# Peer input regrouped by four tokens, read in one, two, four and eight rounds

## The chip, the cores and the metric

The kernel runs on one core of one Trainium2 chip. The metric is the device time of one execution in microseconds. The kernel before takes 1576.94 us (median of three runs, 1575.91 to 1576.96).

## The reference, cut to what matters

Two transformer blocks of width 1024 run over 256 tokens. The first ends with a PEER layer: each of 8 heads picks 16 of 16384 experts per token, and an expert is one row of `peer_u` and one of `peer_v`.

```python
u = peer_u[ec]
a = jax.nn.gelu(jnp.einsum("ckd,cd->ck", u, hc).astype(jnp.float32)) * gc
vv = peer_v[ec]
out = jnp.einsum("ck,ckd->cd", a.astype(vv.dtype), vv)
```

The kernel gathers nothing: it multiplies the normed input `h` by all 16384 rows of `peer_u` (the "scores"), applies gelu, multiplies by gates that are zero for experts not chosen, and then multiplies by all of `peer_v` (the "values").

## The kernel before, in words

**Products.** Every large product is made in three parts with fp32r operands: weights and activations are each split into a rounded part and a rest, and the sum is w_hi x h_hi + w_hi x h_lo + w_lo x h_hi. Weights come from HBM in tiles of 128 x 1024 floats. Two tiles make a chunk, which fills one PSUM bank (`gemm0` to `gemm3`, in rotation). For each tile `product_tile` (L669 to L689) issues 8 matmuls of w_hi with h_hi and 8 with h_lo (L683), then 8 of w_lo with h_hi (L688). In each, the stationary operand is 128 x 128 weights and the moving operand 128 partitions x 256 tokens of one of the 8 parts k of h. A chunk is 48 matmuls.

**Order of the moving operand.** A helper reorders both the moving operand and the PSUM output of every such matmul:

```python
def spread(tile):
    return tile.rearrange("p (j g c) -> p g j c", g=4, c=4)
```

The 256 tokens are taken as 64 groups of four neighbours. The matmul goes through them in 4 rounds of 16 groups, and within a round from every fourth group to the next: 64 bytes on in SBUF and 64 bytes on in PSUM. A group of four floats is 16 bytes. `h_hi` and `h_lo` are two tiles of 8 x 256 floats per partition, so part k begins 1024 bytes after part k-1.

**The scores stage.** There are 64 chunks of `peer_u`. Four chunks, one for each PSUM bank, make one round of a hardware loop (`expert_scores`, L942, for the first 32 chunks; the loop at L970 to L975 for the other 32, in which the small f16 matmuls of `gate_planes`, L966, come before every second chunk). SP loads raw tiles, ACT rounds them to w_hi (L1368) and applies gelu to the finished bank (L1556). The rest w_lo is made by POOL (L466) in the first 32 chunks and by DVE (L466) in the other 32. Each waits by semaphores for the tile before it.

**Where h comes from.** During the eight peer query chunks, which run on another copy (`g_parts`), DVE forms the normed h in `sq` (L2187), ACT rounds it to `h_hi` in four pieces of 128 x 512 (`round_h(1)`, L1322), and DVE subtracts to get `h_lo` in four pieces (`norm2_rest`, L2178). In DVE's queue these subtractions stand between the evacuations of the query banks (L2183); in ACT's queue the roundings stand between roundings of weights. After the query chunks TensorE scores the keys (L936), waits for all pieces of h and starts the scores stage.

Of the kernel before, what the change touches and what calls it, by code (L numbers as in the profile page):

```python
# [30 lines left out]
F32R = mybir.dt.float32r  # L31
# [3 lines left out]
ALU = mybir.AluOpType  # L35
ACT = mybir.ActivationFunctionType
AX = mybir.AxisListType

P = 128
T = 256  # L40
TT = T // P
D = 1024
KD = D // P
# [4 lines left out]
BANKS = 4  # L48
CW = 256
GROUP = 8  # L50
GATE_PARTS = 2
GATE_SCALE = 2.0 ** 14


CONV_W = 31
# [111 lines left out]
def build(nc, t):  # L167
    plan, order = plan_chunks()
    ctx = ExitStack()
    with ctx:  # L170
        def sb(name, shape, dt=F32):
            return ctx.enter_context(nc.sbuf_tensor(name, shape, dt))

        def sem(name):
            return ctx.enter_context(nc.semaphore(name))


        gemm = [ctx.enter_context(nc.psum_tensor(f"gemm{i}", [P, 512], F32)) for i in range(BANKS)]
        aux = [ctx.enter_context(nc.psum_tensor(f"aux{i}", [P, 512], F32)) for i in range(4)]

        def pair(bank, rows=P):
            return bank[0:rows, :].rearrange("p (n t) -> p n t", n=2)
# [3 lines left out]
        w_hi = [sb(f"w_hi{v}", [P, TILE], F32R) for v in range(2)]  # L186
        w_lo = [sb(f"w_lo{v}", [P, TILE], F32R) for v in range(2)]
        xres = sb("xres", [P, KD, T])
        with nc.sbuf_tensor("act_parts", [P, KD, T], F32R) as act_parts:
            pass  # L190
        sb("ahead_of_h", [P, 8])
        h_hi = sb("h_hi", [P, KD, T], F32R)
        with nc.sbuf_tensor("mem_sq", [P, KD, T], F32) as mem_sq:
            pass
        h_lo = sb("h_lo", [P, KD, T], F32R)
        sb("behind_h", [P, 8])
        std = sb("std", [P, T])
        rstd = sb("rstd", [P, T])
        params = sb("params", [P, NPAR])
# [48 lines left out]
        sq = carve(KD, T)  # L248
# [47 lines left out]
            "p b n (g i o) -> p b n g i o", g=GROUP // 2, o=2)  # L296
        hot2 = carve(2, GROUP // 2 * P * 2, dt=F16).rearrange("p b (g i o) -> p b g i o", g=GROUP // 2, o=2)

        a_hi, a_lo = [act_parts[:, i:i + 4, :].rearrange("p (c v) t -> p c v t", c=2) for i in (0, 4)]
        memT = small[:, 0:KD * T].rearrange("p (k t) -> p k t", t=T)  # L300

# [73 lines left out]
        hi_ready = [sem(f"hi_ready{v}") for v in range(2)]  # L375
        lo_ready = [sem(f"lo_ready{v}") for v in range(2)]
        hi_used = [sem(f"hi_used{v}") for v in range(2)]
        tile_done = [sem(f"tile_done{v}") for v in range(2)]
# [53 lines left out]
        def spread(tile):  # L432

            return tile.rearrange("p (j g c) -> p g j c", g=4, c=4)

        def by_k(tile, m, rows=P, n=KD):

            return tile[0:rows, 0:n * m].rearrange("p (k m) -> p k m", m=m)
# [51 lines left out]
        HALF = P // 4  # L490
# [166 lines left out]
        def _(pe):  # L657
            def product(c, m, it=None, x=(h_hi, h_lo), steps=KD):

                for v in range(2):  # L660
                    product_tile(c, v, m, it, x, steps)

            def bank_free(c, it=None):
                if it is not None:
                    pe.wait_ge(evacuated[c.bank], it + (c.bank_use - 1))
                elif c.bank_use > 1:
                    pe.wait_ge(evacuated[c.bank], c.bank_use - 1)
# [23 lines left out]
            def paced_product(c, m, rounded, split, before, x=(h_hi, h_lo), step=2):  # L691


                bank_free(c)
                both = pair(gemm[c.bank], m)
                hi, lo = [by_k(w, m) for w in w_hi], by_k(w_lo[0], m)
# [156 lines left out]
            for k in range(2):  # L853
                mm = pe.matmul(aux[2][:, 0:T], ones[:, :], sq[:, k, :], start=(k == 0), stop=(k == 1))
# [42 lines left out]
            for k in range(KD // 2):  # L897
                mm = pe.matmul(aux[3][:, 0:T], ones[:, :], sq[:, k, :], start=(k == 0), stop=(k == KD // 2 - 1))
# [3 lines left out]
            for j in range(HEADS + 1):  # L902
                if j and j + 1 < HEADS:
                    scores(j + 1)
                if j:
                    turn_probs(j - 1)
                    name, i, v = beside_heads[j - 1]
# [20 lines left out]
            for g in range(TT * 4):  # L928
# [5 lines left out]
                for i in range(4):  # L934
                    v, at = divmod(h0 + i, HALVES // 2)
                    mm = pe.matmul(aux[g % 4][:, i * NK:(i + 1) * NK], qp[:, h0 + i, tt * P:(tt + 1) * P],  # L936
                                   raw[kc.raw][v][:, at * NK:(at + 1) * NK], start=True, stop=True)
# [3 lines left out]

            def expert_scores(first, last):  # L942
                with pe.Fori(first, last) as it:
                    for c in plan["u"][:BANKS]:
                        product(c, P, it)

            pe.wait_ge(h_rounded, 16)
            pe.wait_ge(h_split, 16)
            expert_scores(0, ROUTED + 1)

            pe.wait_ge(gates_ready, 1)
            for n, src in enumerate((e1, e2, sc)):
                for tt in range(TT):
                    mm = pe.transpose(aux[n][:, tt * P:(tt + 1) * P],
                                      src[:, tt].rearrange("p h k -> p (h k)"), ident[:, :])
# [14 lines left out]
            with pe.Fori(0, ITS // 2) as it:  # L970
                for s in range(BANKS):
                    if s % 2 == 0:
                        gate_planes(0, s, it)
                        gate_planes(0, s + 1, it)
                    product(plan["u"][HALF + s], P, it)  # L975

            def expert_values(c, it, opens=False):
                for v in range(2):
# [103 lines left out]
            for h in range(GH):  # L1082
                mm = pe.matmul(pair(aux[h // 2], GDK)[:, h % 2, :], wdec[:, h, :], dec, start=True, stop=True)
# [5 lines left out]
            for h in range(K96):  # L1089
                if h in MQ_TILES:  # L1090
                    n = MQ_TILES.index(h)
# [56 lines left out]
            for tt in range(TT):  # L1148
                for h in range(GH):
                    mm = pe.transpose(aux[tt][:, h * GDK:(h + 1) * GDK], ekd[:, h, tt * P:(tt + 1) * P],  # L1150
                                      ident[0:GDK, 0:GDK])
# [4 lines left out]
            for h in range(GH):  # L1156
                for n in range(NCH):
                    lo, cols = (n % 2) * GCHUNK, slice(n * GCHUNK, (n + 1) * GCHUNK)
                    at_col = (h * TT + n // 2) * GCHUNK
                    mm = pe.matmul(aux[2][lo:lo + GCHUNK, at_col:at_col + GCHUNK], emg[:, h, cols],  # L1160
                                   eg[:, h, cols], start=True, stop=True)
# [99 lines left out]
            for i, c in enumerate(plan["down"]):  # L1261
                pr, g = divmod(i, 3)
# [3 lines left out]
                for v in range(2):  # L1266
                    out = gemm[1][:, 0:T] if pr == 3 and v else pair(aux[pr])[:, v, :]
                    for w, x, ready in ((w_hi, f_hi, hi_ready), (w_hi, f_lo, hi_ready), (w_lo, f_hi, lo_ready)):
                        pe.wait_ge(ready[v], c.split + 1)
                        for k in range(KD):  # L1270

                            mm = pe.matmul(spread(out), w[v][:, k * P:(k + 1) * P], spread(x[:, g * KD + k, :]),  # L1272
                                           start=(g == k == 0 and (v == 0 or pr == 3) and w is w_hi and x is f_hi),
                                           stop=(g == 2 and w is w_lo and k == KD - 1), skip_group_check=True)
# [6 lines left out]
            for part in (0, KD - 1):  # L1281
# [3 lines left out]
                for tt in range(TT):  # L1285
                    mm = pe.matmul(last_sums[:, tt:tt + 1], sq[:, part, tt * P:(tt + 1) * P], ones[:, 0:1],
                                   start=(part == tt == 0), stop=(part == KD - 1), skip_group_check=True)
            mm.then_inc(sumsq, 1)
            keep_warm(3)
            for tt in range(TT):  # L1290
                pe.wait_ge(rstd_done, 7 + tt + 1)
                mm = pe.matmul(last_rstd[:, tt * P:(tt + 1) * P], ones[:, :], spread_rstd[:, tt, :], start=(tt == 0),
                               stop=(tt == TT - 1), skip_group_check=True)
# [4 lines left out]
        def _(act):  # L1298
# [16 lines left out]
            def round_h(j, beside=None):  # L1315

                for q in range(4):
                    part = slice(2 * q, 2 * q + 2)
                    if beside:
                        beside(q)  # L1320
                    act.wait_ge(h_ready, 4 * j + q + 1)
                    act.activation(h_hi[:, part, :], pair(NORMED[q]) if j == 2 else sq[:, part, :],  # L1322
                                   ACT.Copy).then_inc(h_rounded, 1)

# [84 lines left out]
            for n in range(4):  # L1409
                part = slice(2 * n, 2 * n + 2)  # L1410
# [59 lines left out]
            for half in range(2):  # L1470
                part = slice(4 * half, 4 * half + 4)
# [38 lines left out]
            for j in range(HEADS + 3):  # L1510
# [9 lines left out]
                if j in Y_STEPS:  # L1520
                    part = slice(4 * Y_STEPS.index(j), 4 * Y_STEPS.index(j) + 4)
                    act.wait_ge(conv_act, 1)
                    act.activation(y_hi[:, part, :], zv[:, part, :], ACT.Copy).then_inc(y_rounded, 1)
                if j < HEADS:
                    name, i, v = beside_heads[j]
# [10 lines left out]
            for i in range(4):  # L1536
                part = slice(2 * i, 2 * i + 2)
# [130 lines left out]
            c = plan["dec"][0]  # L1668
# [83 lines left out]
            for u in range(MH * QB):  # L1752
# [4 lines left out]
                if u and u % 2 == 0:  # L1757
                    c = plan["gate0"][u // 2 - 1]
# [8 lines left out]
            c = plan["gate0"][-1]  # L1767
# [66 lines left out]
            for i in range(4):  # L1834
                look_ahead(plan["branch1"][i].index + 1)
                act.wait_ge(merge_done, 4 + i + 1)
                part = slice(2 * i, 2 * i + 2)
# [64 lines left out]
        def _(dve):  # L1902
# [227 lines left out]
            for j in range(HEADS + 3):  # L2130
# [6 lines left out]
                if j in Y_STEPS:  # L2137
                    half = Y_STEPS.index(j)
                    part = slice(4 * half, 4 * half + 4)
# [7 lines left out]
                if j >= 11 and j % 2:  # L2147
                    i = (j - 11) // 2
                    c = plan["conv_out"][i]
# [3 lines left out]
                    part = ga[:, 2 * i:2 * i + 2, :]  # L2153
# [21 lines left out]
            def norm2_rest(q):  # L2175
                part = slice(2 * q, 2 * q + 2)
                dve.wait_ge(h_rounded, 12 + q + 1)
                dve.tensor_tensor(h_lo[:, part, :], sq[:, part, :], h_hi[:, part, :], ALU.subtract).then_inc(h_split, 1)  # L2178

            both = rstd[:, :].unsqueeze(1).to_broadcast([P, 2, T])  # L2180
            for i, c in enumerate(plan["peer_q"]):
# [81 lines left out]
            for n, (dst, done) in enumerate(((e1T, planes_used[0]), (e2T, planes_used[1]), (gT, routed))):  # L2263
                dve.wait_ge(routed_psum, n + 1)
                if dst is gT:
                    dve.tensor_scalar(dst, aux[n][:, 0:T], GATE_SCALE, None, ALU.mult).then_inc(done, 1)
                else:
# [32 lines left out]
            def apply_gates(half, s, it):  # L2300
# [3 lines left out]
                                bass.ds(it * (BANKS * GROUP) + GROUP * s, GROUP)]  # L2304
                dve.scalar_tensor_tensor(part, aux[b][:, :].rearrange("p (t i) -> p i t", t=GROUP), 1.0 / GATE_SCALE,  # L2305
                                         part, ALU.mult, ALU.mult).then_inc(planes_used[b], 1)
# [47 lines left out]
            for q in range(4):  # L2354
                part = slice(2 * q, 2 * q + 2)
# [8 lines left out]
            for b in range(BANKS):  # L2364
                dve.wait_ge(experts_turned, b + 1)
                part = xres[:, 2 * b:2 * b + 2, :]
# [287 lines left out]
            for pr in range(3):  # L2654
                taken(dve, plan["down"][3 * pr + 2])
                part = xres[:, 2 * pr:2 * pr + 2, :]
                dve.tensor_tensor(part, part, pair(aux[pr]), ALU.add).then_inc(x4_done, 1)
                gather_squares(6, pr)
            c = plan["down"][-1]
# [15 lines left out]
            for first, last in OUT_TILES:  # L2675
                part = yout[:, first:last, :]
# [92 lines left out]
```

## Time and profile before

| | us |
|---|---|
| median of the runs | 1576.94 |
| the profiled execution's own time | 1579.04 |
| its span (first to last instruction) | 1577.0 |
| TensorE busy | 1561.8 (99%) |
| scores stage, from its first matmul to the first of the values stage | 326.90 to 699.88 |

The profile gives each engine's busy time, groups of instructions by source line, and a chain of waits: it starts at the last instruction and goes back at each step to what released it, or to the instruction before it on the same engine. Where that chain stays on one engine, the time is that engine's own pace, and the length of a piece divided by its instructions is the time from one start to the next. The duration of a single matmul is longer than that, because matmuls overlap.

### The profile page before, as it was taken

The page shows a single profiled execution, that of the slowest core. Times are in us where ns is not written, and L with a number is a line of the kernel's source. Part 1 is how long each engine was busy: PE and PEld are TensorE (multiplying, and loading weights), DVE is VectorE, ACT ScalarE, POOL GpSimd, SP SyncE. Part 2 cuts the span into 40 slices and gives each one's busy share as a digit, 9 for nine tenths or more (in the row PEclk, how much of TensorE's full clock was granted, in tenths as well). Part 3 has the DMA queues.
Part 4 walks back from the last instruction along what each step waited for, and adds up shares of the span by engine and source line. Part 5 has one row for each costly group of instructions (what it writes and reads, how often), then busy time and mean ns, then how long its engine had stood idle before and what let it go on. Part 6 is the DMA issues. An engine that isn't in the chain of part 4 may idle for free.

```text
span 1577.0 us, 33476 instructions
## 1 busy us (share of the span) xinstructions
PE 1561.8 (99%) x12568; PEld 1472.4 (93%) x12568; DVE 1070.0 (68%) x1867; ACT 881.5 (56%) x1251; POOL 883.0 (56%) x413
## 2 busy tenths in 40 slices
PE   9999999999999999999999999999999999999998
PEld 8999899999999999998888888889999999999998
DVE  7998743869933777778888666776937484455522
ACT  5566775554454444444444445557677654676653
POOL 7786458968886000000000244458875689888886
PEclk9999999999999999999999999999999999999999
DMA  6565345656656555555555666666543356666664
GB/s 211 173 199 164 95 134 186 188 181 193 188 186 191 179 164 183 172 166 172 185 177 170 215 195 189 192 202 188 180 140 111 118 165 189 195 195 191 188 193 127
DMA packets 86217, 277.03 MB, mean 176 GB/s; under 512 B 11232, under 2 KB 18160, under 8 KB 86128
## 3 DMA queue, kind: packets, MB, share of 16 engines
q1 hardware_dynamic: 85712, 274.76, 55.8%
q8 instruction: 59, 0.97, 0.3%
q0 software_dynamic: 272, 1.05, 0.2%
q14 instruction: 30, 0.25, 0.1%
q10 hardware_dynamic: 144, 0.00, 0.0%
HBM read 274.73 MB, written 1.05 MB: 175 GB/s over the span
## 4 chain that ended last, share of the span: by engine, by line
PE 91%; POOL 2%; issue 2%; DVE 2%; ACT 2%; DMA 1%; SPq 0%; DVEq 0%; ACTq 0%; POOLq 0%
PE gemm L683 35%; PE gemm L986 22%; PE gemm L688 18%; PE aux L1272 4%; PE gemm L817 3%; PE aux L966 2%; POOL w_lo L466 2%; PE gemm L704 1%; PE gemm L729 1%; ACT w_hi L1368 1%; PE gemm L1272 1%; PE aux L936 0%; PE gemm L803 0%; PE gemm L746 0%; PE gemm L710 0%
## 5 line engine op out<-in xcount | busy, mean ns | idle before, releaser
L466 POOL TENSOR_TENSOR w_lo<-raw,w_hi 128x1024 fp32r<-128x1024 f32 (+1 forms) x330 | 789.7, 2403 | 284.8 <-ACT w_hi L1368 283.9
L1368 ACT ACTIVATE w_hi<-raw 128x1024 fp32r<-128x1024 f32 (+1 forms) x492 | 515.0, 1048 | 560.9 <-PE gemm L683 309.0
L683 PE MATMUL gemm<-h_hi,w_hi 128*128 128x256 f32 x2096 | 289.3, 280 | 1.1 <-ACT w_hi L1368 1.0
L683 PE MATMUL gemm<-h_lo,w_hi 128*128 128x256 f32 x2144 | 289.9, 277 | 0.0
L688 PE MATMUL gemm<-h_hi,w_lo 128*128 128x256 f32 x2096 | 284.4, 277 | 2.6 <-POOL w_lo L466 1.8
L683 PEld LDWEIGHTS gemm<-h_lo,w_hi 128*128 128x128 f32 x2144 | 265.9, 188 | 0.3 <-issue 0.2
L683 PEld LDWEIGHTS gemm<-h_hi,w_hi 128*128 128x128 f32 x2096 | 261.1, 188 | 4.2 <-issue 1.6
L688 PEld LDWEIGHTS gemm<-h_hi,w_lo 128*128 128x128 f32 x2096 | 260.0, 188 | 5.0 <-POOL w_lo L466 3.6
L466 DVE TENSOR_TENSOR w_lo<-raw,w_hi 128x1024 fp32r<-128x1024 f32 x162 | 195.6, 1222 | 101.4 <-ACT w_hi L1368 100.4
L986 PE MATMUL gemm<-w_hi,act_parts 128*128 128x512 f32 x1008 | 249.0, 387 | 0.4 <-ACT act_parts L1569 0.4
L986 PEld LDWEIGHTS gemm<-w_hi,act_parts 128*128 128x128 f32 x1008 | 187.7, 188 | 37.6 <-issue 0.5
L627 POOL DMA_DIRECT2D small<-in_memT x1 | 1.0, 1029 | 379.1 <-DVE big L2305 379.1
L986 PE MATMUL gemm<-w_lo,act_parts 128*128 128x512 f32 x504 | 134.0, 386 | 0.0
L2311 DVE TENSOR_TENSOR act_parts<-big,act_parts 128x512 fp32r<-128x512 f32 x64 | 89.2, 1394 | 47.5 <-ACT act_parts L1569 47.3
L986 PEld LDWEIGHTS gemm<-w_lo,act_parts 128*128 128x128 f32 x504 | 94.4, 187 | 19.5 <-DVE w_lo L466 0.3
L2048 DVE SCALAR_TENSOR_TENSOR aux<-big,params,aux 128x256 f32<-128x256 f32 x240 | 94.8, 506 | 0.0
L462 POOL TENSOR_TENSOR w_lo<-raw,w_hi 128x768 fp32r<-128x768 f32 x30 | 59.2, 1974 | 17.5 <-ACT w_hi L1365 16.7
L2297 DVE TENSOR_TENSOR small<-small 128x512 f16<-128x512 f16 x128 | 57.1, 488 | 0.0
L2614 DVE SCALAR_TENSOR_TENSOR big<-gemm,params,big 128x255 f32<-128x255 f32 (+1 forms) x96 | 39.7, 476 | 24.6 <-ACT big L1851 24.6
L2294 DVE TENSOR_TENSOR small<-small 128x1024 f16<-128x1024 f16 x64 | 43.8, 685 | 0.0
L2305 DVE SCALAR_TENSOR_TENSOR big<-aux,big 128x512 f32 x64 | 41.0, 683 | 0.0
L1569 ACT ACTIVATE act_parts<-big 128x512 fp32r (+1 forms) x64 | 40.0, 627 | 0.2 <-issue 0.2
(436 smaller groups left out, 2047.5 us busy)
## 6 DMA issues: line engine op xcount, KB each, us to landing
raw<-in_w_u SPq DMA_DIRECT2D x128, 512.0 KB, 4.0
raw<-in_w_ev SPq DMA_DIRECT2D x128, 512.0 KB, 3.9
raw<-in_w_up SPq DMA_DIRECT2D x48, 512.0 KB, 4.3
raw<-in_w_gate SPq DMA_DIRECT2D x24, 512.0 KB, 3.8
raw<-in_w_down SPq DMA_DIRECT2D x24, 512.0 KB, 4.3
raw<-in_w_conv_in SPq DMA_DIRECT2D x16, 512.0 KB, 4.4
raw<-in_w_peer_q SPq DMA_DIRECT2D x16, 512.0 KB, 4.3
raw<-in_w_branch SPq DMA_DIRECT2D x24, 288.0 KB, 2.9
```

Source lines behind the costliest of these rows:

```text
L462: eng.tensor_tensor(lo[:, :, 0:C96], by_k(raw[c.raw][v], C96), hi[:, :, 0:C96], ALU.subtract)
L466: eng.tensor_tensor(w_lo[v][:, 0:n], raw[c.raw][v][:, 0:n], w_hi[v][:, 0:n], ALU.subtract).then_inc(lo_ready[v], 1)
L683: mm = pe.matmul(spread(out), w[:, k, :], spread(act_part[:, k, :]), start=(n == k == 0), stop=False)
L688: mm = pe.matmul(spread(out), w[:, k, :], spread(x[0][:, k, :]), start=False, stop=(k == steps - 1))
L817: mm = pe.matmul(spread(pair(gemm[c.bank])[:, tt, :]), x[:, v * KD // 2 + k, tt * P:(tt + 1) * P], spread(w[:, k, :]), start=(begins and t ...
L986: mm = pe.matmul(spread(gemm[2 * half + tt][:, :]), a[:, c.raw, v, tt * P:(tt + 1) * P], spread(w[v][:, half * (D // 2):(half + 1) * (D // ...
L1272: mm = pe.matmul(spread(out), w[v][:, k * P:(k + 1) * P], spread(x[:, g * KD + k, :]), start=(g == k == 0 and (v == 0 or pr == 3) and w is ...
L1368: act.activation(w_hi[v][:, 0:n], raw[c.raw][v][:, 0:n], ACT.Copy).then_inc(hi_ready[v], 1)
L2048: ins = dve.scalar_tensor_tensor(acc, zc[:, k, w:w + T], tap, acc, ALU.mult, ALU.add)
L2294: dve.tensor_tensor(hot2[:, b], each(iota2, P), along(e2T[:, tokens], P), ALU.is_equal)
L2297: ins = dve.tensor_tensor(hot1[:, b, part], hot[:, b], along(gate_parts[:, part, tokens], P // 2), ALU.mult)
L2311: dve.tensor_tensor(a_lo[:, c.raw, :, :], act_peer[:, plane, :], a_hi[:, c.raw, :, :], ALU.subtract).then_inc(a_split, 1)
```

## The change: what it does

The two parts of h for the scores stage get a tile of their own layout, `peer_h`, over the place of `h_hi` and `h_lo`. It has 64 groups, 272 bytes from group to group (`PITCH` 17 x 16 bytes). In a group stand four tokens of h_hi for k = 0 to 7, then four of h_lo for k = 0 to 7, then 16 bytes unused. ACT and DVE write it directly in this order. The spacer behind h grows by 1024 bytes, and what is allocated after it moves by as much.

`score_product` takes the place of `product` in the scores stage. It has the same 48 matmuls in the same sequence with the same waits, but the first, second, third and fourth chunk of each round of the loop go through the 64 groups in 1, 2, 4 and 8 rounds. The steps from group to group are then 272, 544, 1088 and 2176 bytes in SBUF and 16, 32, 64 and 128 bytes in PSUM. Other products keep `spread`.

```diff
+PITCH = 17
+ROUNDS = (1, 2, 4, 8)
...
+        with nc.sbuf_tensor("peer_h", [P, T // 4 * PITCH * 4], F32R) as peer_h:
+            pass
         h_hi = sb("h_hi", [P, KD, T], F32R)
...
-        sb("behind_h", [P, 8])
+        sb("behind_h", [P, 264])
...
+        peer_parts = [peer_h[:, :].rearrange("p (g k c) -> p k g c", k=PITCH, c=4)[:, n * KD:(n + 1) * KD]
+                      for n in range(2)]
...
+            def score_product(c, it, rounds):
+
+                bank_free(c, it)
+                for v in range(2):
+                    out = pair(gemm[c.bank])[:, v, :].rearrange("p (j g c) -> p g j c", g=rounds, c=4)
+
+                    def one(w, part, k, begins=False, ends=False):
+                        moving = peer_parts[part][:, k].rearrange("p (j g) c -> p g j c", g=rounds)
+                        return pe.matmul(out, w[:, k, :], moving, start=begins, stop=ends)
+
+                    pe.wait_ge(hi_ready[v], it * BANKS + (c.split + 1))
+                    for part in range(2):
+                        for k in range(KD):
+                            mm = one(by_k(w_hi[v], P), part, k, begins=(part == k == 0))
+                    mm.then_inc(hi_used[v], 1)
+                    pe.wait_ge(lo_ready[v], it * BANKS + (c.split + 1))
+                    for k in range(KD):
+                        mm = one(by_k(w_lo[v], P), 0, k, ends=(k == KD - 1))
+                    mm.then_inc(tile_done[v], 1)
...
-                    for c in plan["u"][:BANKS]:
-                        product(c, P, it)
+                    for s, c in enumerate(plan["u"][:BANKS]):
+                        score_product(c, it, ROUNDS[s])
...
-                    product(plan["u"][HALF + s], P, it)
+                    score_product(plan["u"][HALF + s], it, ROUNDS[s])
...
+                    if j == 1:
+                        act.activation(peer_parts[0][:, part], sq[:, part, :].rearrange("p k (g c) -> p k g c", c=4),
+                                       ACT.Copy).then_inc(h_rounded, 1)
+                        continue
...
-                dve.tensor_tensor(h_lo[:, part, :], sq[:, part, :], h_hi[:, part, :], ALU.subtract).then_inc(h_split, 1)
+                dve.tensor_tensor(peer_parts[1][:, part], sq[:, part, :].rearrange("p k (g c) -> p k g c", c=4),
+                                  peer_parts[0][:, part], ALU.subtract).then_inc(h_split, 1)
```

## Rows read from the trace of the kernel before

**Rows 1.** The page: span, engines, the chain by engine and by line.
```profile
span 1577.0 us, 33476 instructions
...
PE 1561.8 (99%) x12568; PEld 1472.4 (93%) x12568; DVE 1070.0 (68%) x1867; ACT 881.5 (56%) x1251; POOL 883.0 (56%) x413
...
PE 91%; POOL 2%; issue 2%; DVE 2%; ACT 2%; DMA 1%; SPq 0%; DVEq 0%; ACTq 0%; POOLq 0%
```

**Rows 2.** Windows over the two halves: length, busy (x instructions), clock, DMA, GB/s.
```profile
328.00:506.00 178.00, 177.56 (x1568) 177.13 (x1566) 129.55 (x432) 88.47 (x102) 149.44 (x62) 1.00 0.62 195
506.00:699.00 193.00, 193.00 (x2043) 192.42 (x2039) 144.94 (x223) 84.02 (x96) 0.00 (x0) 1.00 0.54 174
```

**Rows 3.** Waits of TensorE in 328 to 699: total us, times, longest.
```profile
PE gemm L688 <- POOL w_lo L466: 0.4, 2, 0.2
```

**Rows 4.** Chain of waits inside the scores stage: start us, us, what.
```profile
346.96 1.84 PE gemm L683 x16
348.80 0.92 PE gemm L688 x8
349.72 1.84 PE gemm L683 x16
351.56 0.92 PE gemm L688 x8
352.48 1.83 PE gemm L683 x16
...
517.23 0.99 PE aux L966 x32
518.21 1.92 PE gemm L683 x16
520.13 0.92 PE gemm L688 x8
521.05 1.84 PE gemm L683 x16
```

**Rows 5.** Chain of waits, pieces of other stages.
```profile
56.62 3.56 PE gemm L803 x16
...
319.89 7.27 PE aux L936 x64
...
878.43 119.76 PE gemm L986 x528
...
1502.29 52.12 PE aux L1272 x456
```

**Rows 6.** Groups of instructions, 345 to 500: busy us, mean ns, idle before.
```profile
L466 POOL TENSOR_TENSOR w_lo<-raw,w_hi 128x1024 fp32r<-128x1024 f32 x57 | 137.6, 2419 | 20.5 <-ACT w_hi L1368 20.4
...
L1368 ACT ACTIVATE w_hi<-raw 128x1024 fp32r<-128x1024 f32 x56 | 59.3, 1061 | 78.7 <-PE gemm L683 77.5 <-POOL w_lo L466 1.2
```

**Rows 7.** Timeline of DVE before the scores: start us, us, instruction, idle before.
```profile
298.15 0.68 DVE L2178 TENSOR_TENSOR h_lo<-big,h_hi 128x512 fp32r<-128x512 f32 x1
...
303.81 2.88 DVE L2178 TENSOR_TENSOR h_lo<-big,h_hi 128x512 fp32r<-128x512 f32 x1
306.61 0.68 DVE L2183 TENSOR_TENSOR big<-gemm,rstd 128x512 f32<-128x512 f32 x1
...
310.01 2.29 DVE L2178 TENSOR_TENSOR h_lo<-big,h_hi 128x512 fp32r<-128x512 f32 x1
314.39 0.69 DVE L2183 TENSOR_TENSOR big<-gemm,rstd 128x512 f32<-128x512 f32 x1 [2.10 <-PE gemm L688]
319.88 0.69 DVE L2183 TENSOR_TENSOR big<-gemm,rstd 128x512 f32<-128x512 f32 x1 [4.80 <-PE aux L925]
```

**Rows 8.** Timeline of ACT in the same stretch.
```profile
293.20 0.64 ACT L1322 ACTIVATE h_hi<-big 128x512 fp32r<-128x512 f32 x1 [0.56 <-DVE big L2187]
...
297.08 1.06 ACT L1368 ACTIVATE w_hi<-raw 128x1024 fp32r<-128x1024 f32 x1 [1.68 <-PE gemm L683]
```

**Rows 9.** Timeline of TensorE at the start and the end of the scores stage.
```profile
326.90 1.17 PE L683 MATMUL gemm<-h_hi,w_hi 128*128 128x256 f32 x8
```

## The prediction

> **What bounds the kernel now.** Read the page first: TensorE is busy for 99% of the span, and 91% of the chain that ended last is TensorE [rows 1]. Then the two halves of the scores stage, by windows: it is busy for 177.56 of 178 us and for 193.00 of 193 us, at a granted clock of 1.00, which is the 2.4 GHz level; no other engine passes 84% [rows 2]. Then its waits: two, 0.4 us together [rows 3]. So in this stage a change costs or gives what it does to TensorE's own pace, and nothing else unless another engine falls behind.
>
> The pace is in the chain of waits. Sixteen matmuls of L683 take 1.84 us and eight of L688 0.92 us [rows 4], so one 256-column matmul takes 115 ns. 256 columns at one per cycle of 2.4 GHz are 106.7 ns, so 8.3 ns are lost on each. How much of it hangs on the columns? The values stage makes 528 matmuls of 512 columns in 119.76 us [rows 5], 226.8 ns each, 13.5 ns over 213.3. Both read groups of 16 bytes at a 64-byte step; 64 groups lose 8.3 ns and 128 lose 13.5 ns. That makes 5.2 ns per 64 groups, and 3.1 ns that come once per matmul. The 5.2 ns are what the address order can act on.
>
> **The change, part by part.**
>
> *Count.* 64 chunks of 48 matmuls are 3072, 16 chunks or 768 matmuls for each number of rounds. One nanosecond more on all of one kind costs 0.77 us, on all four 3.07 us. No matmul, weight load, wait or DMA is added or taken away in the stage, and the sequence of parts is the same, so weights are released and asked for at the same points.
>
> *Four rounds (third chunk).* The step in PSUM is the present one, 64 bytes. In SBUF it is 1088 bytes, which is 64 beyond four times 256. Taken at nothing. The pace is the same for weights from w_hi with either part of h and for the down projection on another tile at another address (52.12 us for 456, 114.3 ns [rows 5]), which says that where a tile lies matters little. The step itself, at 1088, no row shows.
>
> *One round (first chunk) and two rounds (second).* The steps are 272 and 544 bytes, 16 and 32 beyond a multiple of 256; in PSUM they are 16 and 32 bytes. If the loss depends on how near the next group lies to the last, counted modulo some power of two up to 256, or on how near it lies in PSUM, both chunks go where no row of this trace is: nothing here reads fp32 in one pass at less than a 64-byte step. Bounds for one matmul: from below, the whole 5.2 ns goes (115 to 109.8). From above, the rows with contiguous fp32, which take two passes: 16 records of 256 columns in 3.56 us [rows 5], 222 ns, as if each group took twice as long, 107 ns more. A nearer row for the gain is L936, 64 records in 7.27 us [rows 5]: 113.6 ns for 128 contiguous floats in two passes, with a full 128 x 128 fp32 weight load each. Its operand comes at half the rate, so it should wait for no group, and it is only 1.4 ns faster. So where weights change with each matmul I expect little from an ideal order: 1.4 of the 5.2 ns. For the loss I take the nearest size that is measured, the present loss itself: in one round it doubles (5.2 ns more), in two rounds it grows by half (2.6 ns). 768 x 7.8 ns = 6.0 us. This is a choice close to the low end; the rows with 222 ns are another mode and far away.
>
> *Eight rounds (fourth chunk).* 2176 bytes is 128 beyond a multiple of 256, 128 bytes in PSUM. The same idea has it no nearer than now. Taken at nothing, bounds as above.
>
> *A page against this.* The loss follows the number of 16-byte groups, as worked out from rows 4 and 5. The Trainium skill (SBUF — State Buffer, Specifications (TRN2)) says that SBUF has 16-byte cachelines and that each cross to a new line pays a penalty. By that rule both orders cross after every fourth float, and the sum would be zero instead of 6.0 us. This is the no-change rival below.
>
> *Other engines in the stage.* POOL needs 2 x 2.42 us for a chunk of 5.51 us [rows 6, 4], so it has 0.67 us of air. A slower TensorE widens it. A faster one is covered down to 4.84 us per chunk, 101 ns per matmul, below every bound here. ACT idles 78.7 us of 155 [rows 6]. In the second half DVE is busy 144.94 of 193 [rows 2].
>
> *Writing peer_h.* ACT rounds four pieces, 0.64 us each, into runs of 16 bytes at 272; DVE subtracts four pieces, 0.68 us alone and up to 2.88 us now [rows 7, 8]. No row has this output step, so bound them at nothing and at twice the time. They finish at 312.3, while the first matmul that reads h starts at 326.90 [rows 7, 9]: 14.6 us of cover for the data. Behind the DVE pieces stand the evacuations of the query banks, and the last two of these follow idle times of 2.10 and 4.80 us [rows 7]. ACT's pieces stand among weight roundings that follow 1.68 us of idle time [rows 8]. Doubling 0.64 or 0.68 us fits into both; without that cover it would be at most 4 x 0.64 + 4 x 0.68 = 5.3 us. Taken at nothing.
>
> *The rest.* Tiles behind h move by 1024 bytes. Pace is equal on tiles at many addresses, so this costs nothing.
>
> *Sum.* The profiled execution took 1579.04 us, of which 1577.0 are its span. With 6.0 us added it would take 1585.0; it stood 2.1 us above the median of the runs. From the median: 1576.94 + 6.0 = 1583 us.
>
> **The rivals.**
>
> *No change (1577 us).* The loss is per group whatever the distance, or both operands hide it. For it: equal pace of 114.3 and 115 ns on different tiles, the cacheline rule, and the L936 row. Against it: no row has the same data at another step, so equality over steps is not seen. It holds while the mean over the four kinds moves less than 1.0 ns.
>
> *Faster (1567 us).* The larger steps take the loss away in most chunks. If it goes down to L936's 113.6 ns, 3072 x 1.4 ns = 4.3 us, 1573. If the whole 5.2 ns goes it is 16.0 us, 1561. The middle of the two is 1567. For it: 5.2 ns depend on groups, and every step in SBUF is changed. Against it: L936.
>
> *Faster by contiguous output (1573 us).* One round is the only kind that writes its 256 results one after the other. If the loss comes from jumps in the output, 768 matmuls lose it: 4.0 us less, if the other kinds stay. The L966 matmuls write contiguously and take 0.99 us for 32 of 64 columns [rows 4], 30.9 ns for 26.7 ns of columns, so contiguous output alone does not reach one column per cycle either; this speaks weakly against it. The Trainium skill (PSUM — Partial Sum Buffer, Specifications (TRN2)) says that any non-contiguous access pattern slows matmuls significantly. By that rule the present 64-byte step should hurt much more than it does in rows 4.
>
> *Much slower (1600 us and beyond).* One kind of step lets successive groups collide on the same place, and the stream stops for each. It decides as soon as one kind loses 20 ns per matmul: 15 us. At the 222 ns of the contiguous two-pass rows, one kind would cost 82 us. For it: the steps double from kind to kind, the pattern in which such a collision would show, in eight rounds above all. Against it: the present step is a power of two as well and loses little.
>
> **How the numbers follow.** Forecast as above, slower by some 3 to 12 us: 0.38. Much slower: 0.07. No change: 0.34. Faster in most chunks: 0.15. Faster by contiguous output: 0.06. A measurement of this kernel tells 0.2%, 3.2 us, from no change. The forecast keeps almost all its weight above that bound, so slower is 0.44, same 0.35, faster 0.21. The forecast's own range is 1580 to 1590. Eight in ten: 1570 to 1602, which leaves out the full gain below and the collisions above.
>
> **What would show it.** In the chain of waits a score chunk of 48 matmuls is 5.51 us now. I expect 5.51 + 0.25 = 5.76 us for the first of each four, 5.64 for the second, and 5.51 for the third and fourth. If all four stay at 5.51, no change is right. If the first is shorter and the others equal, output order is the cause. If the third differs from 5.51, the step in SBUF matters on its own, since its step in PSUM is the present one, and my modulo idea is wrong. If TensorE shows waits for DVE, POOL or ACT in the stage or before it, the cover was misjudged. A fourth chunk slower than the third would show that large steps cost something I put at nothing.

## The result and the profile after

The changed kernel takes 1587.38 us (median of 4 runs, 1587.09 to 1587.74), the kernel before 1576.43 us beside it. The ratio is 1.0068, with a 95% interval of 1.0056 to 1.0080. It is slower by 10.95 us, where 6.0 us were forecast.

The page of the changed kernel, its rows that answer to [rows 1]:

```profile
span 1585.5 us, 33476 instructions
...
PE 1571.4 (99%) x12568; PEld 1483.5 (94%) x12568; DVE 1069.0 (67%) x1867; ACT 883.3 (56%) x1251; POOL 883.4 (56%) x413
...
PE 92%; issue 2%; DVE 2%; POOL 2%; ACT 2%; DMA 0%; SPq 0%; DVEq 0%; ACTq 0%; POOLq 0%
```

The instruction counts are the same. TensorE has 9.6 us more busy time and its weight loads 11.1 us; no other engine gained more than 1.8 us. The windows over the halves of the scores stage, as in [rows 2] (length, busy of TensorE, its weight loads, DVE, ACT and POOL, clock, DMA share, GB/s), show it without a gap at the same clock:

```profile
328.00:512.00 184.00, 184.00 (x1574) 183.74 (x1573) 127.66 (x425) 88.32 (x100) 148.96 (x62) 1.00 0.59 190
512.00:709.00 197.00, 197.00 (x2025) 196.28 (x2023) 144.10 (x220) 85.18 (x96) 0.00 (x0) 1.00 0.51 168
```

So the time is in TensorE's own pace. The timeline of TensorE (start us, us, instruction) shows where the stage begins and ends, and one round of the loop: the first row of each of its four chunks, and of the next round.

```profile
325.55 2.14 PE L677 MATMUL gemm<-peer_h,w_hi 128*128 128x256 f32 x16
...
394.00 2.03 PE L677 MATMUL gemm<-peer_h,w_hi 128*128 128x256 f32 x16
...
399.65 2.05 PE L677 MATMUL gemm<-peer_h,w_hi 128*128 128x256 f32 x16
...
405.33 2.01 PE L677 MATMUL gemm<-peer_h,w_hi 128*128 128x256 f32 x16
...
410.86 2.12 PE L677 MATMUL gemm<-peer_h,w_hi 128*128 128x256 f32 x16
...
416.79 1.46 PE L677 MATMUL gemm<-peer_h,w_hi 128*128 128x256 f32 x11
...
709.82 2.02 PE L1012 MATMUL gemm<-w_hi,act_parts 128*128 128x512 f32 x8 [0.41 <-ACT act_parts L1599]
```

The stage lasts 384.27 us (325.55 to 709.82), against 372.98 us before [rows 9 and the table]: 11.3 us more. The chunks with 1, 2, 4 and 8 rounds take 5.65, 5.68, 5.53 and 5.93 us from start to start. Medians over the loop rounds of the first half give 5.656, 5.678, 5.552 and 5.932 us, where every kind took 5.51 before. (A "kind" is the chunks with one number of rounds.) Per matmul (a chunk's time by 48) that is 117.8, 118.3, 115.7 and 123.6 ns against 114.8. Of the four differences, 16 times each, eight rounds make 6.7 us, two rounds 2.7, one round 2.3 and four rounds 0.6. Together they are 12.3 us, 1.0 above the stage's own difference. The trace accounts for most of that rest. In the first half the third and fourth kind alternate from one round of the loop to the next, 5.53 and 5.57 us, 5.93 and 5.86 us, with the same code, so the median of the fourth kind stands too high: a whole round takes 22.76 or 22.79 us against 22.05 before, and sixteen of these differences are 11.6 us. And the kernel before waits twice for POOL in the stage, 0.4 us [rows 3], the changed kernel never: its slower chunks cover that.

In the second half the chain of waits (start us, us, what) shows the same by pairs. The small gate matmuls stand ahead of each pair. The first piece is a pair with four and eight rounds, the last one with one and two; 96 matmuls took 11.11 us before.

```profile
522.40 11.54 PE gemm L677 x96
533.93 0.98 PE aux L992 x32
534.92 11.42 PE gemm L677 x96
```

Writing the new storage cost nothing. These are the rows of DVE and ACT that answer to [rows 7, 8], then two pieces of the chain that answer to [rows 5]:

```profile
302.51 2.87 DVE L2208 TENSOR_TENSOR peer_h<-big,peer_h 128x512 fp32r<-128x512 f32 x1
...
313.04 0.69 DVE L2214 TENSOR_TENSOR big<-gemm,rstd 128x512 f32<-128x512 f32 x1 [2.05 <-PE gemm L714]
318.53 0.69 DVE L2214 TENSOR_TENSOR big<-gemm,rstd 128x512 f32<-128x512 f32 x1 [4.80 <-PE aux L951]
```

```profile
291.87 0.64 ACT L1349 ACTIVATE peer_h<-big 128x512 fp32r<-128x512 f32 x1 [0.58 <-DVE big L2218]
```

```profile
888.43 118.00 PE gemm L1012 x528
...
1510.86 52.11 PE aux L1298 x456
```

DVE takes 2.87 us where it took 2.88, ACT 0.64 as before, and the idle times behind them are 2.05 and 4.80 us where they were 2.10 and 4.80. The down projection is unchanged. The 528 value matmuls took 118.00 us here and 119.76 before, though their code is the same; the last section comes back to it. That and a front part 1.4 us shorter, which wasn't followed up, are why the span grew by only 8.5 us.

### The profile page after: what moved, and what is told of

It is laid out like the page before. It is cut to its first block, busy times and chain, and to the rows that moved or that the text cites. A ratio compares the mean times of both kernels' runs of the same rounds, so it can differ in the third digit from the quotient of the medians.

```text
span 1585.5 us, 33476 instructions
## 1 busy us (share of the span) xinstructions
PE 1571.4 (99%) x12568; PEld 1483.5 (94%) x12568; DVE 1069.0 (67%) x1867; ACT 883.3 (56%) x1251; POOL 883.4 (56%) x413
## 4 chain that ended last, share of the span: by engine, by line
PE 92%; issue 2%; DVE 2%; POOL 2%; ACT 2%; DMA 0%; SPq 0%; DVEq 0%; ACTq 0%; POOLq 0%
PE gemm L677 23%; PE gemm L1012 21%; PE gemm L709 20%; PE gemm L714 11%; PE aux L1298 4%; PE gemm L843 3%; PE aux L992 2%; POOL w_lo L472 1%; PE gemm L730 1%; PE gemm L755 1%; ACT w_hi L1398 1%; PE gemm L1298 1%; PE aux L962 0%; PE gemm L829 0%; PE gemm L736 0%
## 5 line engine op out<-in xcount | busy, mean ns | idle before, releaser
L677 PE MATMUL gemm<-peer_h,w_hi 128*128 128x256 f32 x2048 | 265.1, 282 | 0.0
L677 PEld LDWEIGHTS gemm<-peer_h,w_hi 128*128 128x128 f32 x2048 | 251.6, 189 | 0.0
L709 PE MATMUL gemm<-h_lo,w_hi 128*128 128x256 f32 x1120 | 151.6, 277 | 0.0
L709 PE MATMUL gemm<-h_hi,w_hi 128*128 128x256 f32 x1072 | 149.5, 281 | 1.1 <-ACT w_hi L1398 1.1
L714 PE MATMUL gemm<-h_hi,w_lo 128*128 128x256 f32 x1072 | 146.0, 278 | 2.2 <-POOL w_lo L472 1.3
L677 PE MATMUL gemm<-peer_h,w_lo 128*128 128x256 f32 x1024 | 142.9, 282 | 0.0
L709 PEld LDWEIGHTS gemm<-h_lo,w_hi 128*128 128x128 f32 x1120 | 139.0, 188 | 0.3 <-issue 0.2
L709 PEld LDWEIGHTS gemm<-h_hi,w_hi 128*128 128x128 f32 x1072 | 134.1, 188 | 4.2 <-issue 1.6
L714 PEld LDWEIGHTS gemm<-h_hi,w_lo 128*128 128x128 f32 x1072 | 132.9, 188 | 4.2 <-POOL w_lo L472 2.8
L677 PEld LDWEIGHTS gemm<-peer_h,w_lo 128*128 128x128 f32 x1024 | 130.8, 189 | 0.2 <-POOL w_lo L472 0.2
```

Source lines behind the costliest of these rows:

```text
L677: return pe.matmul(out, w[:, k, :], moving, start=begins, stop=ends)
L709: mm = pe.matmul(spread(out), w[:, k, :], spread(act_part[:, k, :]), start=(n == k == 0), stop=False)
L714: mm = pe.matmul(spread(out), w[:, k, :], spread(x[0][:, k, :]), start=False, stop=(k == steps - 1))
```

## The experiments

All change only the scores stage, and all tell kinds of chunk apart within one run: the four chunks of a loop round carry four variants. The number read from each is the time from chunk to chunk in the first half (median of the loop rounds), given per matmul. It comes from the one profiled execution of each run; the runs whose scores are not the reference's were executed only once. The expectations quote earlier readings of the same kinds, which differ from the final ones by up to 0.4 ns, at 192 bytes by 2.0.

### Output order or input order

The helper got separate numbers of rounds for reading and writing, in the storage of the changed kernel.

```diff
-out = pair(gemm[c.bank])[:, v, :].rearrange("p (j g c) -> p g j c", g=rounds, c=4)
-moving = peer_parts[part][:, k].rearrange("p (j g) c -> p g j c", g=rounds)
+out = pair(gemm[c.bank])[:, v, :].rearrange("p (j g c) -> p g j c", g=out_rounds, c=4)
+moving = peer_parts[part][:, k].rearrange("p (j g) c -> p g j c", g=in_rounds)
```

Reading fixed at 4 rounds, writing in 1, 2, 4, 8:

> Storage of the changed kernel. All chunks read in 4 rounds (1088-byte step); only the order of the output differs, 1, 2, 4, 8 rounds (16, 32, 64, 128 bytes in PSUM). The scores land at permuted tokens, so this is for timing alone. Theory output (PSUM step decides): 118, 118, 115.4, 123.5 ns per matmul by kind. Theory input (SBUF step decides): 115.4 ns in all four kinds.

The same timeline rows of that run:

```profile
393.26 2.00 PE L678 MATMUL gemm<-peer_h,w_hi 128*128 128x256 f32 x16
...
398.80 2.00 PE L678 MATMUL gemm<-peer_h,w_hi 128*128 128x256 f32 x16
...
404.33 2.01 PE L678 MATMUL gemm<-peer_h,w_hi 128*128 128x256 f32 x16
...
409.86 2.00 PE L678 MATMUL gemm<-peer_h,w_hi 128*128 128x256 f32 x16
...
415.40 1.77 PE L678 MATMUL gemm<-peer_h,w_hi 128*128 128x256 f32 x14
```

Four times 5.53 or 5.54 us: 115.3 ns in every kind, and 1578.08 us in all. Writing fixed at 4 rounds, reading in 1, 2, 4, 8:

> The counterpart: all chunks write in 4 rounds (64 bytes in PSUM); the reading goes in 1, 2, 4, 8 rounds (272, 544, 1088, 2176 bytes in SBUF). The scores land at permuted tokens. Theory output: 115.4 ns in all kinds. Theory input: 118, 118, 115.4, 123.5 ns.

```profile
394.39 2.06 PE L678 MATMUL gemm<-peer_h,w_hi 128*128 128x256 f32 x16
...
400.05 2.05 PE L678 MATMUL gemm<-peer_h,w_hi 128*128 128x256 f32 x16
...
405.72 2.03 PE L678 MATMUL gemm<-peer_h,w_hi 128*128 128x256 f32 x16
...
411.30 2.08 PE L678 MATMUL gemm<-peer_h,w_hi 128*128 128x256 f32 x16
...
417.16 1.10 PE L678 MATMUL gemm<-peer_h,w_hi 128*128 128x256 f32 x8
```

117.8, 118.3, 115.2 and 123.6 ns (medians), the changed kernel's pattern, and 1589.28 us in all. The order in which SBUF is read makes the whole difference between the kinds, and the order in PSUM, in runs of 16 bytes, none that can be seen.

### The storage alone, and the rounds alone

```diff
-ROUNDS = (1, 2, 4, 8)
+ROUNDS = (4, 4, 4, 4)
```

> The storage of the changed kernel with 4 rounds in all chunks, that is the storage alone. From the third kind of the changed kernel, 115.4 against 114.8 ns: 3072 x 0.6 = 1.8 us over the kernel before, 1578.3 us. If storage costs nothing and the third kind was only slowed by its neighbours: 1576.5 us. If writing by ACT and DVE costs something, it stands ahead of the scores stage as a wait.

Measured 1579.66 us, ratio 1.0012 (1.0003 to 1.0021), by which it is 1.9 us over the kernel before; 115.3 ns in all kinds against 114.8, and a stage 1.4 us longer (374.4 against 373.0 us). No wait stands ahead of the stage. The storage costs a little by itself. The other way round, the four numbers of rounds on the old storage:

```diff
-peer_parts = [peer_h[:, :].rearrange("p (g k c) -> p k g c", k=PITCH, c=4)[:, n * KD:(n + 1) * KD]
-              for n in range(2)]
+peer_parts = [h[:, :, :].rearrange("p k (g c) -> p k g c", c=4) for h in (h_hi, h_lo)]
```

> The four kinds of chunk (1, 2, 4, 8 rounds) on the storage of the kernel before: h_hi and h_lo apart, a group every 16 bytes, so steps of 16, 32, 64, 128 bytes in SBUF and in PSUM. In the changed kernel the kinds show 118.0, 118.1, 115.4 and 123.5 ns per matmul. Theory A (the step counted modulo 256 bytes, or the output step, decides, and the storage doesn't): again about 118, 118, 115 and 123.5 ns, and the time within 3 us of the changed kernel's 1587.4. Theory B (the far jumps of 272 bytes and more cost by themselves): 1 and 2 rounds fall to 115 or below, 8 rounds as well, 1577 us.

1587.32 us, ratio 1.0062 (1.0046 to 1.0077); 117.3, 117.8, 115.1 and 123.9 ns. So steps of 16, 32, 64 and 128 bytes do what 272, 544, 1088 and 2176 do, within 0.6 ns. It is not the length of the step that makes eight rounds slow. The storage was no part of the loss, up to the 1.4 us above.

### One part undone

```diff
-ROUNDS = (1, 2, 4, 8)
+ROUNDS = (1, 2, 4, 4)
```

> The changed kernel with the fourth kind of chunk in 4 rounds in place of 8, nothing else. By the pace of the kinds, 768 x (123.5 - 115.4) = 6.2 us less than the changed kernel: 1581.2 us, 4.8 above the kernel before (768 x (3.2 + 3.3 + 0.5 + 0.5) = 5.8 by the other way of counting). If the kinds don't add up: over 1584 us.

1583.91 us, against 1579.16 us for the kernel before in the same session: ratio 1.0031 (1.0020 to 1.0043), 4.9 us. The session ran some 2.7 us higher for both, so the absolute figure missed and the difference of 4.8 hit. The kinds add up, and eight rounds are more than half of the loss.

### Which steps are slow

Reading in 4 rounds of 16 groups in every chunk, a round 16 bytes after the last, output as before; only the step is set by hand. `step` counts floats.

```diff
+n = 16 * step
+at = min(k * T, KD * T - n)
+moving = h[:, :, :].rearrange("p k t -> p (k t)")[:, at:at + n].rearrange(
+    "p (j s) -> p j s", s=step)[:, :, 0:16].rearrange("p j (g c) -> p g j c", c=4)
```

> Storage of the kernel before, output as before, 4 rounds of 16 groups in every chunk; only the step from group to group within a round is set by hand, by kind: 80, 96, 192, 256 bytes. A round begins 16 bytes after the last one. The matmuls read overlapping stretches, so the scores are not the reference's; it is for timing. Known so far per matmul: 16 bytes 116.9, 32 bytes 117.8, 64 bytes 114.8 to 115, 128 bytes 123.7 ns. Theory modulo 256 (only the step modulo 256 counts, either direction): 192 is -64, so 115 ns; 80 and 96 between 115 and 124 ns; 256 no move, at least 124 ns. Theory distance (longer steps cost more): 80 < 96 < 192 < 256, the last two above 124 ns. Theory rounds (the number of rounds decides, not the step): all 115 ns.

> The same with steps of 112, 320, 384 and 512 bytes, again with scores that are not the reference's. Modulo 256: 320 = 64 gives 115 ns, 384 = 128 gives 123.7 ns, 512 the same as 256. Modulo 128: 320 gives 115 ns and 384, 512, 256 and 128 are all the same. Modulo 512 or more: 320 and 384 stand apart from 64 and 128. Distance: 320 < 384 < 512, all above 124 ns. Rounds: all 115 ns.

The rows of the second run, with steps of 112, 320, 384 and 512 bytes:

```profile
397.67 1.11 PE L681 MATMUL gemm<-h_hi,w_hi 128*128 128x256 f32 x8
...
403.29 1.08 PE L681 MATMUL gemm<-h_hi,w_hi 128*128 128x256 f32 x8
...
408.80 1.15 PE L681 MATMUL gemm<-h_hi,w_hi 128*128 128x256 f32 x8
...
414.76 1.31 PE L681 MATMUL gemm<-h_hi,w_hi 128*128 128x256 f32 x8
...
421.51 1.11 PE L681 MATMUL gemm<-h_hi,w_hi 128*128 128x256 f32 x8
```

5.62, 5.51, 5.96 and 6.75 us. 320 bytes is as fast as 64 (115.0 ns), 384 as slow as 128 (124.1), and 512 close to 256 (140.5 and 143.3). This fits a modulus of 256 bytes, though 256 and 512 stand 2.8 ns apart where the other pairs agree within 1 ns. It refutes a modulus of 128, under which 384 and 512 would be alike, and a rule by distance. It refutes "rounds decide" as well. The first run, 80, 96, 192 and 256 bytes, took 136.7, 153.3, 117.4 and 143.3 ns, 1645 us in all.

One of these numbers holds for the first half only. The same timeline shows the 192-byte chunk in the first half (from its second group of eight matmuls to the next chunk) and in the second, where the gate matmuls stand ahead of it:

```profile
419.65 1.10 PE L681 MATMUL gemm<-h_lo,w_hi 128*128 128x256 f32 x8
...
424.35 1.31 PE L681 MATMUL gemm<-h_hi,w_hi 128*128 128x256 f32 x8
...
580.98 1.15 PE L996 MATMUL aux<-small 128*128 128x64 f16 x32
...
582.96 1.07 PE L681 MATMUL gemm<-h_lo,w_hi 128*128 128x256 f32 x8
...
587.49 1.31 PE L681 MATMUL gemm<-h_hi,w_hi 128*128 128x256 f32 x8
```

Forty matmuls take 4.70 us in the first and 4.53 us in the second, 117.5 and 113.3 ns, and each value repeats in every round of its half. So the pace hangs not on the step alone but also on what goes before or beside, here by 4 ns; whether the gate matmuls or DVE in POOL's place make it wasn't separated. Every other step of the three step runs keeps its pace within 0.3 ns from half to half.

> As in the other step runs, whole weights, steps of 144, 176, 208, 240 bytes; the scores are not the reference's. If only the step modulo 256 counts and forward and backward are the same, 144 is as 112 (116.7 ns), 176 as 80 (136.8), 240 as 16 (116.9), and 208 is unknown, between them. If direction counts, at least one of the three pairs differs by over 3 ns. A kind below 114.8 ns would be a better order than the present one.

The rows, steps of 144, 176, 208 and 240 bytes:

```profile
397.46 1.08 PE L681 MATMUL gemm<-h_hi,w_hi 128*128 128x256 f32 x8
...
402.92 1.11 PE L681 MATMUL gemm<-h_hi,w_hi 128*128 128x256 f32 x8
...
408.60 1.23 PE L681 MATMUL gemm<-h_hi,w_hi 128*128 128x256 f32 x8
...
414.99 1.14 PE L681 MATMUL gemm<-h_hi,w_hi 128*128 128x256 f32 x8
...
420.83 1.07 PE L681 MATMUL gemm<-h_hi,w_hi 128*128 128x256 f32 x8
```

113.6, 118.4, 133.2 and 121.8 ns (medians). The mirror idea falls: 176 takes 118.4 ns where 80 takes 136.7, and 144 is below 112's 116.9. The step of 144 bytes is faster than the present order by 1.2 ns. The run took 1598.28 us in all. In the table 16, 32 and 128 bytes come from the kinds with 1, 2 and 8 rounds, the others from 4 rounds of 16 groups.

| step, bytes | ns per matmul | | step, bytes | ns per matmul |
|---|---|---|---|---|
| 16 | 117.3 | | 144 | 113.6 |
| 32 | 117.8 | | 176 | 118.4 |
| 64 | 114.8 | | 192 | 117.4, second half 113.3 |
| 80 | 136.7 | | 208 | 133.2 |
| 96 | 153.3 | | 240 | 121.8 |
| 112 | 116.9 | | 256 | 143.3 |
| 128 | 123.9 | | 320 / 384 / 512 | 115.0 / 124.1 / 140.5 |

### Size of the groups

```diff
+ORDERS = ((2, 8), (4, 8), (8, 2), (2, 16))
+tile.rearrange("p (j g c) -> p g j c", g=order[0], c=order[1])
```

> Storage of the kernel before, whole computation kept, moving operand and output in other groups by kind: 32-byte groups at a 64-byte step in 2 rounds; 32-byte groups at 128 bytes in 4 rounds; 8-byte groups at 64 bytes in 8 rounds; 64-byte groups at 128 bytes in 2 rounds. Theory 16-byte unit: what counts is the walk from one 16-byte unit to the next, so larger groups are part 16-byte steps (116.9 ns) and part jumps, between 115 and 121 ns; 8-byte groups visit twice as many units and cost at least 5 ns more. If 32-byte groups at 64 bytes come below 114.8 ns, they are the better order for all products. Time, with 117, 119, 125 and 118 ns by kind: 1576.5 + 0.77 x (2 + 4 + 10 + 3) = 1591 us.

117.7, 117.4, 217.6 and 120.4 ns; 1664.8 us, ratio 1.0552 (1.0535 to 1.0570), where 1591 was expected. The two kinds of 32-byte groups came out near the guess. The 8-byte groups did not: they cost 103 ns more, not 5. Their read goes to a 16-byte unit 128 times per matmul in place of 64, but their output goes in runs of 8 bytes too, which no other run has. That the reads alone nearly double the time is likely and not shown.

### The weight read beside it

First the stationary operand with a step of 4, 8, 16, 32 bytes from column to column, moving operand as in the kernel before:

```diff
+part = w[:, k // step * step * P:(k // step + 1) * step * P]
+w_k = part.rearrange("p (m s) -> p s m", s=step)[:, k % step, :]
```

> Moving operand and output as in the kernel before; only the stationary operand is read with a step: 128 columns at 4, 8, 16 and 32 bytes from column to column by kind, so that the scores are not the reference's. Theory two streams (the loss of a moving read comes from meeting the weight read that runs beside it): the pace changes by kind, and 16 and 32 bytes, with four times the lines, cost 3 ns and more. Theory one stream (the moving read loses by itself): 115 ns in all four kinds.

115.3, 119.9, 233.4 and 242.2 ns; 1770 us. One weight load lasts 188, 198, 329 and 338 ns (medians), where it lasts 188 in the kernel before. With 16 bytes and more, each column lies in a 16-byte unit of its own, and the load, the only thing changed, sets the pace. The step of 8 bytes costs 4.6 ns. That the kinds differ was what "two streams" asked for, but a weight load that is slow by itself explains it as well, so this run doesn't decide. The next two do: the weight read is held on one unit.

```diff
-return pe.matmul(out, w[:, k, :], moving, start=begins, stop=ends)
+return pe.matmul(out, w[:, k, 0:1].to_broadcast([P, P]), moving, start=begins, stop=ends)
```

> Storage of the kernel before, moving operand and output in 1, 2, 4, 8 rounds (16, 32, 64, 128-byte steps), but the stationary operand is one column read 128 times, so the weight read that runs beside the moving read stays on one 16-byte unit; the scores are not the reference's. With whole weights the kinds take 117.0, 117.8, 115.0, 123.7 ns. Theory two streams: the loss is from meeting the weight read, so the kinds fall together at 109 to 111 ns. Theory one stream: the moving read loses by itself, so the four stay apart as they are, within 1 ns.

The rows, moving steps of 16, 32, 64 and 128 bytes:

```profile
394.64 1.07 PE L677 MATMUL gemm<-h_hi,w_hi 128*128 128x256 f32 x8
...
400.08 1.09 PE L677 MATMUL gemm<-h_hi,w_hi 128*128 128x256 f32 x8
...
405.66 1.08 PE L677 MATMUL gemm<-h_hi,w_hi 128*128 128x256 f32 x8
...
411.07 1.08 PE L677 MATMUL gemm<-h_hi,w_hi 128*128 128x256 f32 x8
...
416.66 1.07 PE L677 MATMUL gemm<-h_hi,w_hi 128*128 128x256 f32 x8
```

113.4, 116.3, 112.9 and 116.5 ns (medians) for 117.3, 117.8, 115.1 and 123.9 with whole weights. Both theories miss. The kinds come down by 3.9, 1.5, 2.2 and 7.4 ns, and don't fall together.

> The same stationary column, with the moving steps of 80, 96, 192, 256 bytes that took 136.8, 153.3, 115.4 and 143.4 ns with whole weights. Two streams: 80, 96 and 256 bytes fall by 20 ns or more. One stream: they stay.

137.2, 153.3, 116.2 and 141.3 ns, where whole weights gave 136.7, 153.3, 117.4 and 143.3. The very slow steps are slow by themselves. So there are two parts. A part belongs to the moving read alone, and it makes nearly the whole of what 80, 96 and 256 bytes cost. A part goes away with the walk over the weights, 1.5 to 7.4 ns at steps of 16 to 128 bytes. Of the 8.8 ns between 128 and 64 bytes (123.9 and 115.1), the loss of the eight rounds, 3.6 are left with one column (116.5 and 112.9), and 5.2 go with that walk.

## Why the prediction was right, and which terms were not

**Bound and pace.** Right. TensorE stayed at 100% of both halves, no other engine entered, and the whole loss is pace. The 0.77 us per nanosecond and kind carried the accounting.

**Where the size came from.** In part from luck. The 5.2 ns that price the forecast are the difference between the matmuls of 512 and of 256 columns, with 119.76 us for the 528. The same code took 118.00 us in the changed kernel's trace; by that the difference is 1.8 ns in place of 5.2, and the same working would have given 2.1 us in place of 6.0. Nor is 5.2 ns the limit of what the order can act on: the steps tried run from 113.6 ns (144 bytes) to 153.3 (96 bytes). And 6.7 us of the measured loss stand where the forecast had nothing.

**Four rounds, put at nothing.** 0.4 ns in the run with four rounds everywhere, 0.9 in the changed kernel. A small miss, 0.3 to 0.7 us. By the prediction's own sign a third chunk other than 5.51 us would make the modulo idea wrong. That sign was too sharp: the chunk took 5.53 to 5.57, and 64 bytes on the old storage took 5.52.

**One round and two rounds.** 5.2 and 2.6 ns were taken; 3.0 and 3.5 were measured. Their sum, 7.8 ns forecast, is 6.5 ns: 5.0 us instead of 6.0. The size was nearly right; that one round would cost twice what two do was wrong (5.66 and 5.68 us a chunk, where 5.76 and 5.64 were expected).

**Eight rounds, put at nothing.** This is the failed step. It read "The same idea has it no nearer than now", and the chunk cost 8.8 ns, 6.7 us, more than half of the total. Nor is it that "large steps cost something", as the prediction's last sign has it: 128 bytes on the old storage cost the same as 2176. The idea had two halves. That the step counts modulo 256 bytes is borne out (16 as 272, 128 as 384 and 2176, 64 as 320 and 1088, within 1 ns). That nearness within those 256 bytes makes the loss is refuted: 96 bytes is the slowest step of all and 112 is quick. Without the eight rounds the forecast's 6.0 us would have stood against the 4.9 measured. Why 128 bytes is slow stays open, but for the finding that 5.2 of the 8.8 ns need the walk over the weights.

**The rivals.** No change: refuted. The Trainium skill (SBUF — State Buffer, Specifications (TRN2)) has a penalty for each cross to a new 16-byte line. With the number of lines held at 64, the pace ran from 113.6 to 153.3 ns, so the count alone doesn't set it; the 8-byte groups, which go to a line 128 times, cost 103 ns more, which fits a price per line but was run with their output in runs of 8 bytes too. Faster by contiguous output: refuted. The Trainium skill (PSUM — Partial Sum Buffer, Specifications (TRN2)) says that a non-contiguous pattern slows matmuls significantly. Here fp32 output in 16-byte runs at 16, 32, 64 and 128 bytes took 115.3 ns each time, so no run agrees. Faster in most chunks: no kind was faster. Much slower: it named the right place, eight rounds, but they lost 8.8 ns and not 20; a step of 256 bytes would have lost 28.5 (143.3 against 114.8). That groups collide on one place is not shown, and 96 bytes, which is no doubling, costs more than 256. The rival had 0.07 and no term in the sum.

**Writing and cover.** Right: DVE's and ACT's rows agree within 0.01 us piece by piece.

## What to carry to other kernels

When one matmul stream fills TensorE, the order in which the fp32 moving operand is read is a cost of its own, and four variants in the four slots of a loop measure it in one run to a few tenths of a nanosecond. Read them in both halves, or in another sequence too: one step here was 4 ns faster in the second half, and the third and fourth kind changed by 0.9 and 1.5 ns from one round to the next. Separate the input order from the output order before arguing about either: here output order in 16-byte runs was free, and input order cost up to 38 ns on top of 115. Don't extrapolate from a neighbouring step, and give a step that no row shows its own term, with a price, even where the idea at hand says nothing changes.

## What the runs showed that was not expected

- The pace as a function of the step is neither monotone nor symmetric (80 bytes 136.7 ns, 176 bytes 118.4; 96 bytes 153.3, 112 bytes 116.9). No rule found here explains all rows of the table; the modulus of 256 bytes rests on the pairs named above, and the 192-byte row shows that the step is not all that counts.
- A step of 144 bytes took 113.6 ns, 1.2 under the present 114.8 and near the 1.4 ns that the prediction expected of an ideal order. Over 64 chunks that is 64 x (5.512 - 5.455) = 3.6 us. It was seen only with overlapping reads. A kernel that stores h so that it can be read this way and computes the whole result wasn't tried; it would need other storage, and whether it would beat both kernels is open.
- The values stage comes in two lengths in the profiled executions, with the same code: 361.2 to 361.3 us in seven of them (the changed kernel among them) and 362.8 to 363.1 us in the other seven (the kernel before among them). 528 of its matmuls take 118.00 or 119.7 us, at a granted clock of 1.00 both times. The cause is open; it makes single spans differ by 1.7 us, so small differences here want several runs.
